# Mixers: the sliding attention's weights moved first, background steps spread over the half units, attended rows multiplied ahead of the recurrent ones

## The chip, the cores and the metric

The kernel runs on one core of a Trainium2 chip. The metric is the time of one execution on the device in microseconds (us); lower is better. Names of engines: PE is TensorE's matmul, DVE is VectorE, ACT is ScalarE, POOL is GpSimd, SP is the queue that issues the transfers.

## What is computed

Two blocks of a language model over 256 positions of width 1024, in float32. The change touches one sublayer of the second block, the mixers: one projection of the normed rows gives the inputs of a sliding window attention and of a gated recurrence, and both results are projected, gated and added.

```python
proj = u @ w_in[layer]
aq, ak, av, rq, rf, ri, rg, ga, gb = jnp.split(proj, splits, axis=-1)
att = sliding_window_attention(aq, ak, av, rel_bias, attn_sinks[layer])   # 8 heads on 2 key heads, window 128
rec = hgrn2_recurrence(rq, rf, ri, lower_bounds[layer])                   # 4 heads, f = lb + (1-lb)*sigmoid(rf)
rec = rms_norm(rec, rec_norm[layer]).reshape(B, S, REC_V_W) * jax.nn.sigmoid(rg)
y_a = att @ w_att_proj[layer]
y_b = rec @ w_rec_proj[layer]
merged = jax.nn.sigmoid(ga) * y_a + jax.nn.sigmoid(gb) * y_b
h = h + merged @ w_out[layer]
```

## The kernel before

All weights stream through the core once, as 528 half units of 128x1024 numbers. A float32 product is made of three matmuls of rounded parts (high by high, high by low, low by high), so each half unit is split first: ACT copies it to `whi` (line 634), DVE subtracts to get `wlo` (line 1109). There are four slots for split half units (`NSPLIT`), so the split of half unit v+3 starts when PE has finished half unit v-1 (`Ahead.upto`). One half unit of the usual kind is 24 matmuls (line 1799).

The mixers begin at half unit 398. Counted from there, in the kernel before: 0 to 3 give the forget gates f of the recurrence, 4 to 7 its queries q, 8 to 11 the attention's queries aq, 12 and 13 its keys ak and values av, 14 to 17 the recurrence's values ii (12 matmuls of 512 columns each), 18 to 37 are ten pairs of gates (`sgm`, `sgr`), 38 to 45 project both results, and 46 to 53 are `w_out`. A pair of half units fills one bank of PSUM, and ACT evicts it when both are done (sigmoid for f and the gates, copy for the others); DVE turns the sigmoid of f into f and 1-f (lines 1718 and 1720).

Beside these run three background tasks: `recurrence()` (on DVE scans, then sixteen rounds of `pp` at line 1605 and `gg` at line 1608, whose `pp` PE sums by the matmuls with `eo_t` at line 1802), `sliding()` (four rounds: PE scores, DVE adds the bias and takes maxima, ACT exponentials at line 989, DVE normalizes at line 1688, PE transposes at line 2281, ACT copies them at line 998, PE multiplies by the values, ACT and DVE store `hhi` and `hlo` at lines 1003 and 1694), and `later()` (the recurrence's states, its output, the norm at line 1648 and the gate at line 1656). Each engine has its own generator of every task; a call `bg.fill(n)` advances the tasks in turn by n steps, and the generators are written so that step number k means the same on each engine. ACT and DVE call `bg.fill` after they have split what `half_unit(v)` asks for, that is half unit v+3:

```python
def half_unit(u, n=1):
    use(u)
    ahead.done = u
    bg.fill(n)
```

PE calls it where the text says. In `pair()` of the kernel before that is behind each of the two half units, and in the loop over the gates four more behind the pair, on all engines alike. What is left of the tasks when the last pair is done is drained by `bg.drain()`, with no matmuls of weights between, and then the projections start: for each output tile 12 matmuls with the attended rows `hhi`/`hlo` and 12 with the recurrent ones `xhi`/`xlo`, which wait for `m_rlo`.

Of the kernel before, what the change touches and what calls it, by code (L numbers as in the profile page):

```python
# [134 lines left out]
def program(nc, w, rows, cols, pT, b1c, ssm_s, ssm_b, ssm_c, ssm_cc, oh, idn, eo, x, out, scr):  # L135
# [4 lines left out]
    with ctx:  # L140
# [484 lines left out]
        def scalar(a):  # L625
# [293 lines left out]
            def mixers():  # L919
                v0, done = [MIX_AT], set()  # L920

                def pair():
                    half_unit(v0[0])
                    half_unit(v0[0] + 1)
                    v0[0] += 2
                    return v0[0]
# [82 lines left out]
                for j in range(2):  # L1009
                    q.wait_ge(s_used, pair())  # L1010
                    a.activation(fq[:, 2 * j:2 * j + 2, :], two(pair_bank(n)), ACT.Sigmoid).then_inc(m_sf, 1)
                    n += 1
                for j in range(2):
                    q.wait_ge(s_used, pair())
                    a.activation(qq[:, 2 * j:2 * j + 2, :], two(4 + n % 2), ACT.Copy)
                    a.activation(gg[:, 2 * j:2 * j + 2, :], two(4 + n % 2), ACT.Copy).then_inc(m_q, 1)
                    n += 1
                bg.add(recurrence())
                for j in range(2):
                    q.wait_ge(s_used, pair())  # L1020
                    a.activation(turned(flat4(aq[:, 2 * j:2 * j + 2, :])), in128(PS[:, 4 + n % 2, :]), ACT.Copy).then_inc(m_aq, 1)
                    n += 1
# [9 lines left out]
                bg.add(sliding())  # L1032
                for c in range(4):
                    half_unit(v0[0], 2)
                    v0[0] += 1
# [4 lines left out]
                for j in range(8):  # L1040
                    while j < 2 and "d" not in done:
                        bg.fill()
                    if j in (4, 6):
                        q.wait_ge(s_used, pair())
# [3 lines left out]
                    q.wait_ge(s_used, pair())  # L1048
# [50 lines left out]
        def vector(v):  # L1099
# [442 lines left out]
            def mixers():  # L1542
                v0, done = [MIX_AT], set()

                def pair():
                    half_unit(v0[0])
                    half_unit(v0[0] + 1)
                    v0[0] += 2
# [163 lines left out]
                v.memset(s_eo[:, 63:64], 0.0).then_inc(m_zero, 1)  # L1712
                for j in range(2):
# [12 lines left out]
                half_unit(v0[0])  # L1726
                half_unit(v0[0] + 1, 0)
                v0[0] += 2
                bg.add(sliding())
                for c in range(4):  # L1730
                    half_unit(v0[0], 2)
                    v0[0] += 1
                bg.add(later())
                for j in range(8):
                    while j < 2 and "d" not in done:
                        bg.fill()
                    if j in (4, 6):
                        pair()
                        bg.fill(4)
                    pair()  # L1740
                    bg.fill(4)
                done.add("rg")
# [51 lines left out]
        def tensor(pe):  # L1794
# [59 lines left out]
            def half_unit(u, o):  # L1854
# [5 lines left out]
                e.then_inc(s_used, 1)  # L1860
# [287 lines left out]
            def mixers():  # L2148
                u0, done, nb = [MIX_AT], set(), [0]

                def bank_free(n):

                    n -= 2
                    if n >= 0:
                        s, c = ((m_sf, n + 1) if n < 2 else (m_q, n - 1) if n < 4 else (m_aq, n - 3) if n < 6 else
                                (m_ak, 1) if n == 6 else (m_av, 1) if n == 7 else None) if n < 8 else (
# [3 lines left out]
                def pair():  # L2160
                    b = pair_bank(nb[0])
                    bank_free(nb[0])
                    nb[0] += 1
                    if nb[0] == 1:
                        first_half_unit(u0[0], PS[:, b, 0:S], 9)
                    else:
                        half_unit(u0[0], PS[:, b, 0:S])
                    bg.fill()
                    half_unit(u0[0] + 1, PS[:, b, S:2 * S])
                    bg.fill()  # L2170
                    u0[0] += 2

                def recurrence():
                    for i in range(7):
# [122 lines left out]
                for _ in range(4):  # L2297
                    pair()
                q.wait_ge(l_eo, 16)
                q.wait_ge(m_f, 8)  # L2300
                q.wait_ge(m_zero, 1)
                mm(PS[:, 3, 0:S], zero.to_broadcast([128, 128]), fq[:, 0, :], True, True)
                bg.add(recurrence())
# [4 lines left out]
                bg.fill()  # L2308
# [14 lines left out]
                bg.add(sliding())  # L2323
                for c in range(4):
# [10 lines left out]
                    e.then_inc(s_used, 1)  # L2335
                    bg.fill(2)
                bg.add(later())
                for j in range(8):
                    while j < 2 and "d" not in done:
                        bg.fill()  # L2340
                    if j in (4, 6):
                        pair()
                        bg.fill(4)
                    pair()
                    bg.fill(4)
                done.add("rg")
                bg.drain()
                for j in range(8):
                    hi, lo = (z.rearrange("p (m k n) -> p m k n", m=2, k=4) for z in weight(u0[0]))
                    u0[0] += 1  # L2350
                    b = 4 + j % 4
                    if j < 2:
                        q.wait_ge(m_sg, 7 + j)
                    elif j >= 4:
                        q.wait_ge(m_gm, j - 3)
                    q.wait_ge(a_ol, 12)
                    for m, (ahi, alo) in enumerate(((hhi, hlo), (xhi, xlo))):
                        if m:
                            q.wait_ge(m_rlo, 1)
                        o = PS[:, b, S * m:S * m + S]  # L2360
                        for k in range(4):
                            mm(o, hi[:, m, k, :], ahi[:, k, :], k == 0, False)
                            mm(o, hi[:, m, k, :], alo[:, k, :], False, False)
                            e = mm(o, lo[:, m, k, :], ahi[:, k, :], False, k == 3)
                    e.then_inc(s_used, 1)
# [36 lines left out]
def pack(i):  # L2402
# [42 lines left out]
    for m in (rf, rq):  # L2445
        for j in range(2):
            ws(cut(m, 2 * j), cut(m, 2 * j + 1))
# [3 lines left out]
    ws(ak, av)  # L2451
    rows_(ri, 512)
# [86 lines left out]
```

## Time and profile before

| | before |
|---|---|
| median of 3 runs | 1823.16 us (1822.29 to 1826.94) |
| the profiled execution | 1826.12 us, span 1824.3 us |
| mean granted clock of TensorE | 0.984 |
| PE busy | 1734.6 us (95%) |
| DVE busy | 1090.7 us (60%) |
| ACT busy | 881.3 us (48%) |
| first matmul of the mixers' half units | 1360.04 us |
| first matmul of the projections | 1532.10 us |

The profiled execution took 1826.12 us by the clock of the runs; the span is what the trace covers of it, from its first instruction to its last. Times of the trace count from the span's start. Busy shares are shares of the span. The granted clock is 1 at 2.4 GHz and 0.5 at 1.2 GHz.

### The profile page before, as it was taken

The numbers are of one execution on the slowest core, as the hardware profiler recorded it, in microseconds if no ns is written. First come the engines' busy times: TensorE is split into PE (matmuls) and PEld (weight loads), VectorE is DVE, ScalarE is ACT, GpSimd is POOL, SyncE is SP. The second block draws the span as 40 slices with busy tenths as digits, with TensorE's granted clock in tenths as the row PEclk, the third lists the DMA queues.
The fourth block names the chain that finished last, engine by engine and source line by source line (L and its number), as shares of the span: only waits on it lengthen the run. The fifth ranks groups of instructions, "written<-read, shape, count | busy, mean of one in ns | idle before, by whom it ended". The sixth has DMA issues, their size and how long they took to land.

```text
span 1824.3 us, 28207 instructions
## 1 busy us (share of the span) xinstructions
PE 1734.6 (95%) x11999; PEld 1588.3 (87%) x11999; DVE 1090.7 (60%) x1410; ACT 881.3 (48%) x1370; POOL 166.6 (9%) x192
## 2 busy tenths in 40 slices
PE   7999999999998999999999998999999997999996
PEld 6899799899977998989789997899989887899994
DVE  5455567678766544658565555655566575655554
ACT  5344466544564455453454445544454444444443
POOL 0000001218001002800000000000000000000000
PEclk9999999999999999999999999999999998999998
DMA  6655433454544544531445554465544331455551
GB/s 226 237 188 187 178 139 139 160 190 179 199 158 153 182 170 143 185 116 47 184 155 176 187 199 146 163 221 184 185 159 177 122 111 70 158 206 185 185 185 69
DMA packets 51086, 300.99 MB, mean 165 GB/s; under 512 B 6073, under 2 KB 12689, under 8 KB 17169
## 3 DMA queue, kind: packets, MB, share of 16 engines
q1 hardware_dynamic: 50800, 298.66, 45.7%
q8 instruction: 95, 1.56, 0.3%
q0 software_dynamic: 160, 0.52, 0.1%
q14 instruction: 31, 0.25, 0.0%
HBM read 298.08 MB, written 1.09 MB: 164 GB/s over the span
## 4 chain that ended last, share of the span: by engine, by line
PE 75%; ACT 9%; DVE 7%; DMA 3%; issue 2%; POOL 1%; SPq 1%; DVEq 0%; ACTq 0%; POOLq 0%
PE PS L1799 72%; DVE wlo L1109 3%; ACT whi L634 3%; DMA raw<-in_w 2%; PE PS L1802 2%; ACT wk L677 2%; POOL st L526 1%; DVE xn L1194 1%; ACT SC L766 1%; PE PS L1919 1%; DVE X L1186 1%; ACT SC L854 1%; DMA SC<-in_pT 0%; POOL st L519 0%; PE PS L2099 0%
## 5 line engine op out<-in xcount | busy, mean ns | idle before, releaser
L1109 DVE TENSOR_TENSOR wlo<-raw,whi 128x1024 fp32r<-128x1024 f32 x528 | 661.3, 1262 | 445.3 <-ACT whi L634 444.5
L634 ACT ACTIVATE whi<-raw 128x1024 fp32r<-128x1024 f32 x528 | 549.7, 1053 | 412.6 <-PE PS L1799 254.3
L1799 PE MATMUL PS<-xhi,whi 128*128 128x256 f32 x2536 | 724.9, 286 | 5.8 <-DVE wlo L1109 5.2
L1799 PE MATMUL PS<-xhi,wlo 128*128 128x256 f32 x2536 | 719.3, 284 | 0.0
L1799 PE MATMUL PS<-xlo,whi 128*128 128x256 f32 x2536 | 710.3, 283 | 0.0
L1799 PEld LDWEIGHTS PS<-xhi,whi 128*128 128x128 f32 x2536 | 489.6, 193 | 14.1 <-DVE wlo L1109 7.0
L1799 PEld LDWEIGHTS PS<-xhi,wlo 128*128 128x128 f32 x2536 | 489.7, 193 | 0.0
L1799 PEld LDWEIGHTS PS<-xlo,whi 128*128 128x128 f32 x2536 | 484.2, 192 | 2.0
L1799 PE MATMUL PS<-whi,hhi 128*128 128x512 f32 x544 | 170.2, 394 | 2.5 <-DVE wlo L1109 2.5
L1799 PE MATMUL PS<-wlo,hhi 128*128 128x512 f32 x544 | 168.5, 391 | 0.0
L1799 PE MATMUL PS<-whi,hlo 128*128 128x512 f32 x544 | 168.3, 390 | 0.0
L716 ACT ACTIVATE wk<-PS 128x256 f32<-128x256 f32 x132 | 50.3, 381 | 164.1 <-PE PS L1799 163.9
L1799 PEld LDWEIGHTS PS<-wlo,hhi 128*128 128x128 f32 x544 | 102.4, 188 | 22.1
L1799 PEld LDWEIGHTS PS<-whi,hlo 128*128 128x128 f32 x544 | 102.4, 188 | 22.0
L1799 PEld LDWEIGHTS PS<-whi,hhi 128*128 128x128 f32 x544 | 98.1, 190 | 19.1 <-DVE wlo L1109 2.7
L1230 DVE TENSOR_TENSOR wk<-PS,wk 128x256 f32<-128x256 f32 x132 | 55.8, 422 | 87.4 <-ACT wk L716 87.3
L519 POOL TENSOR_SCALAR st<-st 128x1 f32<-128x1 f32 x36 | 11.4, 318 | 1055.9 <-ACT wk L677 546.6
L720 ACT ACTIVATE hhi<-wk 128x256 fp32r<-128x256 f32 x132 | 55.2, 418 | 95.8 <-DVE wk L1230 95.8
L1232 DVE TENSOR_TENSOR hlo<-wk,hhi 128x256 fp32r<-128x256 f32 x132 | 58.8, 446 | 63.9 <-ACT hhi L720 63.9
L1799 PE MATMUL PS<-whi,xhi 128*128 128x512 f32 (+2 forms) x272 | 90.5, 391 | 6.2 <-DVE wlo L1109 5.7
L1799 PE MATMUL PS<-wlo,xhi 128*128 128x512 f32 (+2 forms) x272 | 88.1, 382 | 0.0
L1799 PE MATMUL PS<-whi,xlo 128*128 128x512 f32 (+2 forms) x272 | 80.0, 371 | 0.0
(261 smaller groups left out, 1454.7 us busy)
## 6 DMA issues: line engine op xcount, KB each, us to landing
raw<-in_w SPq DMA_DIRECT2D x264, 1024.0 KB, 4.8
gr<-in_rows SPq DMA_DIRECT2D x23, 512.0 KB, 3.8
SC<-scratch SPq DMA_DIRECT2D x1, 2048.0 KB, 12.1
SC<-scratch SPq DMA_DIRECT2D x2, 1024.0 KB, 11.7
X<-in_x SPq DMA_DIRECT2D x2, 512.0 KB, 4.9
xn<-in_sc SPq DMA_DIRECT2D x2, 512.0 KB, 6.8
out<-xn SPq DMA_DIRECT2D x2, 512.0 KB, 2.7
SC<-in_pT SPq DMA_DIRECT2D x3, 256.0 KB, 4.1
```

What stands on the lines that cost most here:

```text
L526: g.tensor_tensor(r, ms, mh[:, 0:max(n, 1)], ALU.pow).then_inc(done, 1)
L634: a.activation(whi[:, u % NSPLIT, :], raw[:, u // 2 % NRAW, u % 2 * HU:u % 2 * HU + HU], ACT.Copy).then_inc(s_hi, 1)
L677: a.activation(wk[:, f], X[:, h, f], ACT.Square, scale=1 / 32, accum_out=ss[:, i:i + 1]).then_inc(s_sq, 1)
L716: a.activation(sg[:, f % 2, :], PS[:, b, 0:S], ACT.Silu).then_inc(s_silu, 1)
L720: a.activation(hhi[:, f % 4, :], hf[:, f % 2, :], ACT.Copy).then_inc(s_hhi, 1)
L766: e = a.activation(pr[:, m, l:z], sc[:, m, l:z], ACT.Exp, bias=n4[:, m, c:c + 1], accum_out=s4[:, m, c:c + 1])
L854: e = a.activation(cst[r, k, :, s, 16 * i:16 * i + 16], o[k][r], ACT.Copy)
L1109: v.tensor_tensor(wlo[:, u % NSPLIT, :], src, hi.bitcast(f32), SUB).then_inc(s_lo, 1)
L1230: v.tensor_tensor(hf[:, f % 2, :], PS[:, up_bank(f), S:2 * S], sg[:, f % 2, :], MUL).then_inc(s_hm, 1)
L1232: v.tensor_tensor(hlo[:, f % 4, :], hf[:, f % 2, :], hhi[:, f % 4, :].bitcast(f32), SUB).then_inc(s_hlo, 1)
L1799: return pe.matmul(o, l, r, start=start, stop=stop)
L1802: return pe.matmul(o, l, r, start=False, stop=True, skip_group_check=True)
```

## The change

The half units of the mixers come in another order (the weights are packed so on the host): aq, ak and av first (0 to 5), then f (6 to 9), q (10 to 13), ii (14 to 17), and the rest as before. `sliding()` is added to the background after half unit 5 and `recurrence()` after the f pairs. From then on there are two background steps in each half unit instead of one, three in each half unit of ii instead of two, and in the loop over the gates three in each half unit and one behind the pair (seven a pair where there were six). On PE they no longer stand behind the half unit but within it. After the loop PE multiplies the attended rows of three output tiles before it waits for the recurrent ones.

```diff
 def mixers():
-    def pair():
-        half_unit(v0[0])
-        half_unit(v0[0] + 1)
+    def pair(a=2, b=2):
+        half_unit(v0[0], a)
+        half_unit(v0[0] + 1, b)
...
     for c in range(4):
-        half_unit(v0[0], 2)
+        half_unit(v0[0], 3)
...
-                        bg.fill(4)
-                    q.wait_ge(s_used, pair())
+                        bg.fill()
+                    if j == 6:
+                        done.add("rg")
+                    q.wait_ge(s_used, pair(3, 3))
...
-                    bg.fill(4)
-                done.add("rg")
+                    bg.fill()
...
-            def half_unit(u, o):
+            def half_unit(u, o, fills=()):
...
                 for k in range(8):
                     mm(o, hi[:, k, :], xhi[:, k, :], k == 0, False)
                     mm(o, hi[:, k, :], xlo[:, k, :], False, False)
                     e = mm(o, lo[:, k, :], xhi[:, k, :], False, k == 7)
-                e.then_inc(s_used, 1)
+                    if k == 7:
+                        e.then_inc(s_used, 1)
+                    if k in fills:
+                        bg.fill()
...
-                def pair():
+                def pair(a=(3, 7), b=(3, 7)):
...
-                for _ in range(4):
-                    pair()
...
-                bg.add(recurrence())
                 pair()
                 pair()
...
                 bg.add(sliding())
+                pair()
+                pair()
+                bg.add(recurrence())
+                pair()
+                pair()
...
                     if j in (4, 6):
-                        pair()
-                        bg.fill(4)
-                    pair()
-                    bg.fill(4)
-                done.add("rg")
+                        pair((2, 5, 7), (1, 3, 5))
+                        bg.fill()
+                    if j == 6:
+                        done.add("rg")
+                    pair((2, 5, 7), (1, 3, 5))
+                    bg.fill()
                 bg.drain()
...
+                q.wait_ge(a_ol, 12)
+                for j in range(3):
+                    if j < 2:
+                        q.wait_ge(m_sg, 7 + j)
+                    projected(j, 0)
+                q.wait_ge(m_rlo, 1)
+                for j in range(8):
+                    if j >= 4:
+                        q.wait_ge(m_gm, j - 3)
+                    if j > 2:
+                        projected(j, 0)
+                    projected(j, 1).then_inc(s_used, 1)
```

First place: DVE, from the split of the last queries on. L1109 is the split of a half unit, L1718 and L1720 make f and 1-f, L1559 begins the recurrence. Before, splits stand with nothing between them and then the recurrence begins:

```order
L1718 TENSOR_SCALAR SC<-SC,st 128x256
L1720 TENSOR_SCALAR SC<-SC 128x256
L1109 TENSOR_TENSOR wlo<-raw,whi 128x1024 x5
L1559 COPY wk<-SC 128x1024
L1561 MEMSET wk 128x64
```

In the changed kernel, where lines are one higher up to the sliding task and seven higher behind it in DVE's mixers, the softmax of the first sliding round (L1684 to L1689) stands between the two pairs of f:

```order
L1110 TENSOR_TENSOR wlo<-raw,whi 128x1024
L1684 TENSOR_TENSOR st<-st 128x4
L1686 RECIPROCAL st<-st 128x4
L1689 TENSOR_TENSOR SC<-SC,st 128x2x256
L1689 TENSOR_TENSOR SC<-SC,st 128x2x128
L1110 TENSOR_TENSOR wlo<-raw,whi 128x1024
L1725 TENSOR_SCALAR SC<-SC,st 128x256
L1727 TENSOR_SCALAR SC<-SC 128x256
```

The first sliding round thus shares DVE and ACT with the gates f, where it stood before beside ii and the first gates.

Second place: PE at the end of the mixers' background. Before, these rows stand between the last gate matmul and the first projection (L2281 transposes of the sliding task, L2256 of the recurrence's output, L1802 its sums):

```order
L1799 MATMUL PS<-xhi,wlo 128x256
L2281 MATMUL PS<-idt,SC 128x128 x6
L1802 MATMUL PS<-SC 128x128 x4
L1799 MATMUL PS<-SC 64x128 x6
L1799 MATMUL PS<-SC 128x256
L1799 MATMUL PS<-SC 128x128
L1799 MATMUL PS<-SC 128x256
L1799 MATMUL PS<-SC 128x128
L2256 MATMUL PS<-idt,xn 128x128 x8
L2281 MATMUL PS<-idt,SC 128x128 x6
L1799 MATMUL PS<-SC 64x128 x6
L1799 MATMUL PS<-hhi,whi 128x256
```

In the changed kernel the last background row of PE (L2264 is L2256 of before) has gate matmuls on both sides, and 54 more follow before the projections:

```order
L1801 MATMUL PS<-xhi,whi 128x256
L1801 MATMUL PS<-xlo,whi 128x256
L1801 MATMUL PS<-xhi,wlo 128x256
L2264 MATMUL PS<-idt,xn 128x128 x4
L1801 MATMUL PS<-xhi,whi 128x256
L1801 MATMUL PS<-xlo,whi 128x256
```

Nothing is left for the drain there.

Third place: PE in the second half unit of a gate pair. A sum of the recurrence (L1804 with `eo_t`) stood behind the 24 matmuls; now it stands behind the sixth or twelfth of them, or in the first half unit of a pair behind the ninth, eighteenth or last:

```order
L1801 MATMUL PS<-xhi,wlo 128x256
L1804 MATMUL PS<-SC,eo_t 32x8x2 x8
L1801 MATMUL PS<-xhi,whi 128x256
L1801 MATMUL PS<-xlo,whi 128x256
L1801 MATMUL PS<-xhi,wlo 128x256
```

This one stands behind the twelfth. On DVE the operation that it waits for stands where it stood, behind the split of the half unit three further on.

## Rows read from the trace of the kernel before

**Rows 1.** The page, first part: busy time of each engine.

```profile
PE 1734.6 (95%) x11999; PEld 1588.3 (87%) x11999; DVE 1090.7 (60%) x1410; ACT 881.3 (48%) x1370; POOL 166.6 (9%) x192
```

**Rows 2.** Busy time by stretch: stretch, its length, PE, PEld, DVE, ACT, POOL, clock, DMA.

```profile
1360.04:1513.31 153.27, 149.12 (x1403) 138.00 (x1403) 101.88 (x162) 71.96 (x108) 0.00 (x0) 0.98 0.38 134
1513.31:1532.10 18.79, 9.13 (x63) 7.07 (x61) 7.88 (x22) 8.90 (x34) 1.85 (x2) 0.73 0.01 1
```

**Rows 3.** Timeline of PE, the drain: start, length, and idle time before with its releaser.

```profile
1524.12 1.12 PE L2256 MATMUL PS<-idt,xn 128*128 128x128 f32 x4 [3.29 <-DVE xn L1648]
...
1532.10 0.55 PE L1799 MATMUL PS<-hhi,whi 128*128 128x256 f32 x1 [1.03 <-DVE hlo L1694]
```

**Rows 4.** Timeline of PE, its other waits in the mixers.

```profile
1422.73 0.60 PE L2208 MATMUL PS<-idt,xn 128*128 128x128 f32 x4
1425.38 0.34 PE L1802 MATMUL PS<-SC,eo_t 128*32 128x8 f32 x16 [2.05 <-DVE SC L1605]
...
1467.99 0.51 PE L1802 MATMUL PS<-SC,eo_t 128*32 128x80 f32 x16 [0.67 <-DVE SC L1605]
...
1509.48 0.79 PE L1802 MATMUL PS<-SC 128*128 128x128 f32 x5 [1.44 <-DVE SC L1638]
```

**Rows 5.** The chain that ended last: two half units of 24 matmuls.

```profile
1426.52 4.36 PE PS L1799 x24
1431.15 3.07 PE PS L1799 x24
```

**Rows 6.** Timeline of ACT.

```profile
1416.92 0.21 ACT L986 ACTIVATE st<-st 128x4 f32<-128x4 f32 x1 [0.94 <-DVE st L1680]
...
1418.79 1.05 ACT L1038 ACTIVATE SC<-PS 128x512 f32<-128x512 f32 x2
...
1463.10 1.28 ACT L1045 ACT_TABLE_LOAD   x1
...
1477.92 1.06 ACT L634 ACTIVATE whi<-raw 128x1024 fp32r<-128x1024 f32 x1 [3.84 <-PE PS L1799]
```

**Rows 7.** Timeline of DVE.

```profile
1367.43 0.41 DVE L1718 TENSOR_SCALAR SC<-SC,st 128x256 f32<-128x256 f32 x1 [0.59 <-ACT SC L1011]
...
1368.74 1.22 DVE L1109 TENSOR_TENSOR wlo<-raw,whi 128x1024 fp32r<-128x1024 f32 x1
...
1399.21 2.29 DVE L1579 TENSOR_TENSOR_SCAN xn<-wk,SC 128x1024 f32<-128x1024 f32 x1
...
1424.11 1.03 DVE L1688 TENSOR_TENSOR SC<-SC,st 128x512 f32<-128x512 f32 x2
...
1479.01 1.23 DVE L1109 TENSOR_TENSOR wlo<-raw,whi 128x1024 fp32r<-128x1024 f32 x1 [0.56 <-ACT whi L634]
1480.15 1.02 DVE L1605 TENSOR_TENSOR SC<-SC 128x832 f32<-128x832 f32 x1
...
1486.73 1.08 DVE L1605 TENSOR_TENSOR SC<-SC 128x896 f32<-128x896 f32 x1
```

**Rows 8.** Timeline of PE: background steps behind half units of the gates.

```profile
1477.75 0.56 PE L1802 MATMUL PS<-SC,eo_t 128*32 128x96 f32 x16
...
1481.30 1.15 PE L1799 MATMUL PS<-SC 128*64 128x128 f32 x12
...
1488.03 0.61 PE L1802 MATMUL PS<-SC,eo_t 128*32 128x112 f32 x16
```

**Rows 9.** Groups by line: busy us, mean ns; the sixteen `pp` operations.

```profile
L1605 DVE TENSOR_TENSOR SC<-SC 128x64 f32<-128x64 f32 (+15 forms) x16 | 11.5, 721 | 0.0
```

**Rows 10.** The projections: second output tile on PE, splits on DVE.

```profile
1536.65 0.28 PE L1799 MATMUL PS<-hhi,whi 128*128 128x256 f32 x1
1536.77 0.28 PE L1799 MATMUL PS<-hlo,whi 128*128 128x256 f32 x1
...
1539.43 1.23 DVE L1109 TENSOR_TENSOR wlo<-raw,whi 128x1024 fp32r<-128x1024 f32 x1 [0.52 <-ACT whi L634]
...
1558.03 1.23 DVE L1109 TENSOR_TENSOR wlo<-raw,whi 128x1024 fp32r<-128x1024 f32 x1 [0.52 <-ACT whi L634]
```

More of the change, by code:

```diff
@@ L1010, in mixers @@
                     q.wait_ge(s_used, pair())
[L1011 to L1021 removed]
+                    a.activation(turned(flat4(aq[:, 2 * j:2 * j + 2, :])), in128(PS[:, pair_bank(n), :]), ACT.Copy).then_inc(m_aq, 1)
                     n += 1
@@ L1032, in mixers @@
                 bg.add(sliding())
+                for j in range(2):
+                    q.wait_ge(s_used, pair())
+                    a.activation(fq[:, 2 * j:2 * j + 2, :], two(4 + n % 2), ACT.Sigmoid).then_inc(m_sf, 1)
+                    n += 1
+                bg.add(recurrence())
+                for j in range(2):
+                    q.wait_ge(s_used, pair())
+                    a.activation(qq[:, 2 * j:2 * j + 2, :], two(4 + n % 2), ACT.Copy)
+                    a.activation(gg[:, 2 * j:2 * j + 2, :], two(4 + n % 2), ACT.Copy).then_inc(m_q, 1)
+                    n += 1
                 for c in range(4):
-                    half_unit(v0[0], 2)
+                    half_unit(v0[0], 3)
                     v0[0] += 1
@@ L1712, in mixers @@
                 v.memset(s_eo[:, 63:64], 0.0).then_inc(m_zero, 1)
+                pair()
+                pair()
+                half_unit(v0[0])
+                half_unit(v0[0] + 1, 0)
+                v0[0] += 2
+                bg.add(sliding())
                 for j in range(2):
@@ L1725, in mixers @@
                 pair()
[L1726 to L1729, printed above, removed]
                 for c in range(4):
-                    half_unit(v0[0], 2)
+                    half_unit(v0[0], 3)
                     v0[0] += 1
@@ L2295, in sliding @@
                         yield
-                for _ in range(4):
[L2298 to L2303, printed above, removed]
                 pair()
@@ L2323, in mixers @@
                 bg.add(sliding())
+                pair()
+                pair()
+                bg.add(recurrence())
+                pair()
+                pair()
                 for c in range(4):
@@ L2341, in mixers, with projected @@
                     if j in (4, 6):
[L2342 to L2346, printed above, removed]
-                bg.drain()
[L2348 to L2351, printed above, removed]
+                        pair((2, 5, 7), (1, 3, 5))
+                        bg.fill()
+                    if j == 6:
+                        done.add("rg")
+                    pair((2, 5, 7), (1, 3, 5))
+                    bg.fill()
+                bg.drain()
+                def projected(j, m):
+                    hi, lo = (z.rearrange("p (m k n) -> p m k n", m=2, k=4)[:, m] for z in weight(u0[0] + j))
+                    ahi, alo = ((hhi, hlo), (xhi, xlo))[m]
+                    o = PS[:, 4 + j % 4, S * m:S * m + S]
+                    for k in range(4):
+                        mm(o, hi[:, k, :], ahi[:, k, :], k == 0, False)
+                        mm(o, hi[:, k, :], alo[:, k, :], False, False)
+                        e = mm(o, lo[:, k, :], ahi[:, k, :], False, k == 3)
+                    return e
+                q.wait_ge(a_ol, 12)
+                for j in range(3):
                     if j < 2:
                         q.wait_ge(m_sg, 7 + j)
-                    elif j >= 4:
+                    projected(j, 0)
+                q.wait_ge(m_rlo, 1)
+                for j in range(8):
+                    if j >= 4:
                         q.wait_ge(m_gm, j - 3)
[L2356 to L2365, printed above, removed]
+                    if j > 2:
+                        projected(j, 0)
+                    projected(j, 1).then_inc(s_used, 1)
                 q.wait_ge(m_rec, 2)
@@ L2451, in pack @@
     ws(ak, av)
+    for m in (rf, rq):
+        for j in range(2):
+            ws(cut(m, 2 * j), cut(m, 2 * j + 1))
     rows_(ri, 512)
```

40 lines of the change are left out of this document (20 added, 20 removed).

## The prediction

> **What bounds the kernel now.** I read the page first: PE is busy 95% of the span, DVE 60%, ACT 48% [rows 1]. So what counts is when PE waits or runs at half clock; work of the others counts where PE waits for it. Then the busy time by stretch. The mixers up to the projections take 172.1 us, from 1360.0 to 1532.1, of which the last 18.8 are the drain, where PE is busy 9.13 us at a mean clock of 0.73 [rows 2]. The timeline of PE shows who is late there: the longest wait, 3.29 us, is for DVE's norm, the last for `hlo` [rows 3]. 9.13 us at 0.73 are 6.7 us of work at full clock, so the drain loses 18.8 - 6.7 = 12.1 us. The first output tile behind it is still slow: it takes 1536.65 - 1532.10 = 4.55 us [rows 3, 10] where 24 matmuls without a background step take 2.88 (0.12 us from one to the next [rows 10]; with a step behind them 3.07 [rows 5]), so 1.7 more. Before the drain PE waits only three times: 2.05, 0.67 and 1.44 us [rows 4]; behind the first, 24 matmuls took 4.36 instead of 3.07 us [rows 5], so that wait costs 3.3. The change can win back 12.1 + 1.7 + 3.3 + 0.7 + 1.4 = 19.2 us at most.
>
> **The change part by part.**
>
> *The drain* goes: PE's last background step now stands before the last 54 gate matmuls. Behind the loop the recurrent rows need ACT's eviction of the last gate (0.5), `xhi` (about 1.06, as a `whi` of the same size [rows 6]), and `xlo` (1.2, as a `wlo` [rows 7]), 3.2 us with the handovers; the 36 attended matmuls put ahead of them take 4.3 us. So no wait: the cover has 1.1 us to spare. I count all 19.2 us as won.
>
> *More interruptions.* A background step among 24 matmuls costs 3.07 - 2.88 = 0.18 us beside its own work. In the order of before 21 places on PE have background work between weight matmuls (the drain apart), in the changed order 43. 22 x 0.18 = 4.0 us lost. No matmul is added or removed otherwise, no transfer is moved to another place of SP's queue, and ACT loads its tables as often (nine times in the mixers).
>
> *First sliding round.* Let S be the start of half unit 6, where it now begins. PE: scores behind 12 matmuls, done at S+2.4; half unit 6 ends at S+3.9 and 8 at S+9.7, where the transposes stand. DVE and ACT: the bias is added by S+3.5 (768 elements, 0.95 us as 832 take 1.02 [rows 7]); then DVE splits half unit 10, which waits for the end of 6: `whi` begins 0.17 us behind it (1477.92 against 1477.75) [rows 6, 8] and lasts 1.06, `wlo` lets DVE go 1.14 later (1479.01 to 1480.15) [rows 7], so 2.4 us behind a half unit's end, S+6.3. Maxima and sink, 1.4: S+7.75. Exponentials, 1.87 (1416.92 to 1418.79) [rows 6]: S+9.7. Behind them ACT's queue has the sigmoid of the first f pair with its table, 1.28 [rows 6] and 0.5 (half of a `whi`'s 1024 elements): S+11.5, and DVE's queue has the four operations on f, 1.31 (1367.43 to 1368.74) [rows 7], then the split of 11 (1.14), and only then the softmax, 1.4 with its last 1.03 [rows 7]: S+15.4, on PE S+15.7. PE waits 6.0 us. Before, this softmax ended at 1425.1 [rows 7], behind half unit splits and two evictions, and PE's 2.05 us of wait [rows 4] were for the same queue; its transposes then stood twice as many matmuls behind the scores. A wait of 2.05 was followed by 1.3 us of half clock [rows 4, 5]; I add that: 7.3.
>
> *Second sliding round*, now beside the recurrence's scans. From the start of half unit 12 DVE has: split of 15 behind an eviction 3.35, bias 0.9, scan 2.3, split 1.15, maxima 0.95, copies 0.9, split 1.15, sink 0.4, memsets and second scan 2.6 (its 2.29 [rows 7]), softmax 1.4, in all 15.1 us. PE reaches the transposes, in half unit 15, behind 2 x 2.88 + 2.84 + 2.13 = 10.7 us. It waits 4.6, and 1.3 for the clock: 5.9. Rounds three and four have more steps between, and I find no wait there.
>
> *The sixteen rounds of the recurrence.* This is the largest term. Round k needs `pp` of k, 0.27 to 1.22 us (mean 0.72 [rows 9]). DVE gets to it 2.4 us behind the end of the half unit before (2.9 where ACT evicts a pair first), behind whatever background step comes ahead of it there. In the kernel before PE is never there sooner: in the first half unit of a pair it comes behind 24 matmuls and some 3 us of steps that follow the pair (1481.30 to 1488.03, with `pp` done at 1487.8) [rows 7, 8]; the spare is 0.2 us. In the changed kernel PE is there 1.2, 2.4 or 3.0 us into the first half unit, or 0.8, 1.5, 2.3 or 3.0 into the second. Example: round 11 stands behind six matmuls of a second half unit, at 0.8; DVE: 2.4 + 0.88 + 0.06 = 3.35; PE waits 2.55. Followed round by round through the order with these durations, the waits are 0.45, 1.5, 2.15, 2.05, 0, 0, 0.4, 0, 1.95, 1.55, 2.55, 0, 1.8, 0.55, 0.95, 0: together 15.9. Then the copies of A3 (1.5, as now 1.44 [rows 4]) and the norm of the recurrence's output, now 30 matmuls behind its product where squares, POOL and norm need 5 to 6 us: 2.0. Sum 19.4 us. The bounds: 0, if DVE is always ready; 16 x 2.55 + 3.5 = 44, if every round waits as long as the worst. I take the walk's value, since each of its terms is a duration of a row.
>
> *Projections.* The first three tiles now end 1.44 us apart, the first at 4.3 + 1.44 = 5.8 us. Per tile DVE takes (1558.03 - 1539.43)/5 = 3.72 us and splits half unit 42 by 4.0 us behind the first tile's end [rows 10]; so half unit 47 is split at 5.8 + 4.0 + 5 x 3.72 = 28.4, and PE wants it at 8 x 2.88 + 2.84 = 25.9: 2.5 us lost. (Before, the first tile ended at 4.55 and PE wanted it 1.7 later, which just fitted.)
>
> *Sum*: -19.2 + 4.0 + 7.3 + 5.9 + 19.4 + 2.5 = **+19.9 us**. Against the profiled execution's 1826.1 that is 1846; the median of the runs lies 3.0 below it, so 1843. About 0.3%, 5.5 us, is what a measurement of this kernel can tell from no change.
>
> **The rivals.**
>
> *The steps are ready in time* (faster). Were all new waits zero, the sum would be -19.2 + 4.0 = -15.2, or -12.7 with the projections' 2.5: 1808 to 1811. For it: DVE is busy 102 of 153 us in the stretch and PE waits 4 us there [rows 2]. Against: DVE's free time lies before its split, which waits for PE. It decides below 12.7 us of new waits, against my 7.3 + 5.9 + 19.4 = 32.6. Chance 0.1.
> The Trainium skill, Perfetto Trace Analysis, Optimization Strategy, says that interleaving regimes with different contended engines may improve performance; by that this rival is what happens. Rows 2 and 3 agree that the drain is such a regime, and no row here says that the interleaving stays free.
>
> *Both halves cancel* (same). The first two sliding waits come but the recurrence's are a third of mine, or the reverse: 1818 to 1828. Chance 0.09.
>
> *The clock falls too* (slower still). Seven of my waits in the gates are 1.5 us or more, and a wait of 2.05 was followed by half clock while one of 1.44 was not [rows 4, 5]. At 1.3 each: +9, 1852. For it: they come one or two a pair. Against: slow matmuls give DVE time, so part of it shortens the next wait. Chance 0.18.
> The Trainium skill, TensorE: Matmul & The Clock Gate, A second HAM failure mode, says that frequent short idles between groups of matmuls can make the clock swing between its levels; by that the 1852 would be the forecast. The drain's 0.73 agrees, the stretch before it with 0.98 holds no such group of waits.
>
> *My forecast*, 1834 to 1848: chance 0.63.
>
> **How the numbers follow.** Faster is the first rival, 0.1; within 0.3% the second, 0.09; slower the other two, 0.81. The likeliest one's range is 1834 to 1848. For 8 in 10 it reaches up into the clock rival, 1855, and down through the cancelling one to 1822, since both bounds of the largest term are far off.
>
> **What would show it.** After the change PE's timeline should have no drain: gate matmuls up to the first `hhi` one, and no wait on `m_rlo`. It should have a wait of about 6 us for the softmax at the first sliding transposes, one of 3 to 5 at the second, and some ten waits of 0.4 to 2.6 us for `pp` inside half units of the gates, the mean clock there below 0.98. From the first matmul of the mixers to the first projection some 189 us instead of 172. Wrong would be: DVE's splits sooner behind a half unit's end than 2.4 us, or `pp` done before PE's ninth matmul. The step I trust least is the size of the recurrence's term.

## The result and the profile after

The changed kernel took 1850.6 us (median of 4 runs, 1845.63 to 1853.69) against 1824.42 for the kernel before beside it: ratio 1.014, 95% interval 1.011 to 1.0171, so 26.2 us slower. The forecast was 1843, likeliest 1834 to 1848, range 1822 to 1855. The profiled execution took 1853.69 us, span 1851.9.

First the sections of the page on busy time, and the waits of PE from the mixers' first matmul to the first projection (who waited for whom: us in total, times, longest), of the changed kernel:

```profile
PE 1744.5 (94%) x11999; PEld 1592.2 (86%) x11999; DVE 1090.1 (59%) x1410; ACT 878.8 (47%) x1369; POOL 166.6 (9%) x192
...
PE PS L1804 <- DVE SC L1606: 14.6, 11, 2.6
PE PS L2289 <- DVE SC L1689: 10.0, 2, 5.9
PE PS L2264 <- DVE xn L1649: 2.2, 1, 2.2
PE PS L1804 <- DVE SC L1639: 1.8, 1, 1.8
```

The counts are those of [rows 1], ACT's less one (a table load: eight in the mixers, where the prediction had nine as before); PE is busy 10 us longer with the same 11999 matmuls. The drain is gone, and 28.6 us of waits stand in the mixers, where before 4.2 stood ahead of the drain ([rows 4]) and 9.7 in it. Busy time by stretch, with the columns of [rows 2]:

```profile
1360.11:1440.00 79.89, 69.48 (x569) 64.28 (x568) 47.66 (x79) 36.84 (x61) 0.00 (x0) 0.93 0.35 125
1440.00:1500.00 60.00, 48.68 (x454) 42.38 (x445) 29.15 (x51) 19.75 (x31) 0.00 (x0) 0.87 0.25 88
1500.00:1560.44 60.44, 53.53 (x453) 48.12 (x451) 32.43 (x57) 21.26 (x47) 1.85 (x2) 0.93 0.22 78
1560.44:1610.32 49.88, 47.12 (x295) 41.63 (x293) 32.96 (x44) 21.01 (x29) 0.85 (x2) 1.00 0.50 181
```

From the first matmul to the first projection the mixers take 200.33 us (1360.11 to 1560.44) instead of 172.06; the forecast was 189. The granted clock, 0.98 up to the drain in [rows 2], is 0.87 to 0.93 over all three stretches. Behind the first projection 49.88 us follow to the next sublayer's first transposes; before they were 48.64. How the clock falls is to be seen in the timeline of PE, second half of a gate pair:

```profile
1444.53 0.34 PE L1804 MATMUL PS<-SC,eo_t 128*32 128x16 f32 x16 [1.67 <-DVE SC L1606]
...
1447.18 0.28 PE L1801 MATMUL PS<-xlo,whi 128*128 128x256 f32 x1
1447.31 0.28 PE L1801 MATMUL PS<-xhi,wlo 128*128 128x256 f32 x1
1449.67 0.35 PE L1804 MATMUL PS<-SC,eo_t 128*32 128x24 f32 x16 [2.08 <-DVE SC L1606]
...
1450.43 0.42 PE L1801 MATMUL PS<-xhi,whi 128*128 128x256 f32 x1
1450.64 0.42 PE L1801 MATMUL PS<-xlo,whi 128*128 128x256 f32 x1
1450.86 0.41 PE L1801 MATMUL PS<-xhi,wlo 128*128 128x256 f32 x1
...
1453.83 0.28 PE L1801 MATMUL PS<-xhi,whi 128*128 128x256 f32 x1
1453.94 0.28 PE L1801 MATMUL PS<-xlo,whi 128*128 128x256 f32 x1
...
1457.38 0.42 PE L1801 MATMUL PS<-xlo,whi 128*128 128x256 f32 x1
1457.60 0.41 PE L1801 MATMUL PS<-xhi,wlo 128*128 128x256 f32 x1
```

Up to the second wait one matmul follows the other by 0.12 to 0.13 us, 0.7 us behind it by 0.21 to 0.22: the lower level of the clock. From 1453.83 the distance is 0.12 again, and behind the next wait, of 2.09 us up to 1456.79, it is 0.21 to 0.22 once more. So the level comes and goes with the waits. What PE waits for is in the chain that ended last (start, length, what):

```profile
1451.92 0.85 PE PS L2216 x4
1452.77 1.23 PE PS L1801 x6
...
1454.08 1.07 ACT whi L634
...
1455.21 1.11 issue
1456.32 0.43 DVE SC L1606
...
1456.79 0.36 PE PS L1804 x14
```

PE ends a half unit, ACT and DVE split the next but two into the slot that came free, then DVE makes `pp`, then PE goes on: the loop of 2.4 us plus `pp` that the prediction walked through. (The 1.11 of "issue" are the split by DVE, L1110 in its timeline.)

### The profile page after: what moved, and what is told of

The parts are those of the page before. It is cut to its first block, busy times and chain, and to the rows that moved or that the text cites. A ratio compares the mean times of both kernels' runs of the same rounds, so it can differ in the third digit from the quotient of the medians.

```text
span 1851.9 us, 28207 instructions
## 1 busy us (share of the span) xinstructions
PE 1744.5 (94%) x11999; PEld 1592.2 (86%) x11999; DVE 1090.1 (59%) x1410; ACT 878.8 (47%) x1369; POOL 166.6 (9%) x192
## 4 chain that ended last, share of the span: by engine, by line
PE 67%; DVE 11%; ACT 10%; DMA 5%; issue 4%; POOL 1%; SPq 1%; DVEq 0%; ACTq 0%; POOLq 0%
PE PS L1801 64%; DVE wlo L1110 5%; ACT whi L634 4%; DMA raw<-in_w 4%; PE PS L1804 2%; ACT wk L677 2%; DVE xn L1195 1%; POOL st L526 1%; ACT SC L766 1%; PE PS L1925 1%; DMA SC<-in_pT 1%; DVE X L1187 1%; DVE SC L1348 1%; ACT SC L854 1%; DVE wk L1231 0%
## 5 line engine op out<-in xcount | busy, mean ns | idle before, releaser
L1110 DVE TENSOR_TENSOR wlo<-raw,whi 128x1024 fp32r<-128x1024 f32 x528 | 661.4, 1262 | 485.7 <-ACT whi L634 484.6
```

What stands on the lines that cost most here:

```text
L1110: v.tensor_tensor(wlo[:, u % NSPLIT, :], src, hi.bitcast(f32), SUB).then_inc(s_lo, 1)
```

## The experiments

Each kernel was timed against the kernel before on its own chip; its ratio holds against that. "Stretch" is the time from the mixers' first matmul to the first projection in the profiled execution, which is one execution out of several: the changed kernel's took 3.1 us more than its median, those of fill_gates and fill_all 3.0 and 4.1 us less than theirs. Their mixers also begin 4.0 us sooner, which the stretch leaves out. So where a stretch carries a conclusion, the ratio stands beside it.

| kernel | median us | ratio, 95% interval | stretch us | waits for `pp` us |
|---|---|---|---|---|
| before | 1824.42 | 1 | 172.06 | 2.7 |
| changed | 1850.6 | 1.014 [1.011, 1.0171] | 200.33 | 14.6 |
| late_round | 1829.54 | 1.0029 [1.0016, 1.0042] | 173.33 | 1.3 |
| steps_behind | 1827.71 | 1.0015 [1.0, 1.0029] | 175.29 | 4.0 |
| order_only | 1839.66 | 1.0084 [1.0054, 1.0113] | 186.65 | 14.3 |
| fills_only | 1849.97 | 1.0141 [1.0118, 1.0164] | 199.54 | 16.2 |
| order_turned | 1831.11 | 1.0032 [1.0019, 1.0045] | 177.54 | 10.5 |
| late_slow | 1824.75 | 1.0002 [0.9991, 1.0014] | 170.09 | 0.6 |
| late_both | 1829.26 | 1.0027 [1.0016, 1.0038] | 174.48 | 3.9 |
| hh_only | 1826.76 | 1.0011 [1.0001, 1.0021] | 171.26 | 2.7 |
| fill_gates | 1845.6 | 1.0114 [1.0099, 1.013] | 192.63 | 3.3 |
| fill_all | 1842.59 | 1.0093 [1.0077, 1.0108] | 188.82 | 3.3 |
| late_tail | 1829.85 | 1.0027 [1.0017, 1.0037] | 172.80 | 2.6 |
| slow_old | 1824.45 | 0.9994 [0.9982, 1.0006] | 171.59 | 0.6 |

**Are the recurrence's rounds the loss?** The changed kernel with one empty step of PE more ahead of its sixteen rounds, so that each sum stands a turn of the tasks (18 to 24 matmuls) further behind its `pp`:

```diff
                     done.add("B")
                     yield
+                    yield
                     for s in range(15, -1, -1):
```

> The changed kernel with one more empty step on PE ahead of the recurrence's sixteen rounds, so that PE sums a round one turn of the tasks (21 matmuls, 2.5 us, and the steps between) later than DVE makes its pp; nothing is left out. My theory (PE meets each round sooner than DVE's queue can reach it, behind the split of the half unit three further on): the 14.6 us of waits for pp in the gates fall below 2 us, and most of the half clock in the gates goes with them (some 8 us), so about 1828 us, 1822 to 1835. Rival a (the clock is low in the gates because of the two sliding waits ahead of them): waits fall by 14, the clock does not change, about 1837. Rival b (DVE is simply short of time there and the waits come back at the next thing it owes): 1845 or more.

Measured: ratio 1.0029, 21 us of the 26 back. PE's waits and the stretches of the gates:

```profile
PE PS L2290 <- DVE SC L1689: 10.0, 2, 5.9
PE PS L1804 <- DVE SC L1606: 1.3, 1, 1.3
PE PS L1804 <- DVE SC L1639: 1.0, 1, 1.0
PE PS L2265 <- DVE xn L1649: 1.0, 1, 1.0
...
1360.93:1440.00 79.07, 69.02 (x557) 64.03 (x558) 47.76 (x79) 36.86 (x61) 0.00 (x0) 0.91 0.36 127
1440.00:1500.00 60.00, 58.68 (x628) 51.72 (x627) 42.18 (x76) 28.23 (x47) 0.00 (x0) 1.00 0.29 106
1500.00:1534.26 34.26, 32.20 (x283) 29.56 (x281) 19.06 (x32) 12.83 (x31) 1.85 (x2) 1.00 0.33 114
```

The waits of rounds, copies and norm fall by 15.3 us (18.6 to 3.3), the stretch by 27.0, and the clock in the gates is 1.00. So some 12 us come from more than the waits. The sliding waits (10.0 us) stay, as they must.

**Is it the place within the half unit, or the number of steps?** The same steps at the same half units, but all behind them on PE:

```diff
-                def pair(a=(3, 7), b=(3, 7)):
+                def pair(a=(7, 7), b=(7, 7)):
...
-                    pair((2, 5, 7), (1, 3, 5))
+                    pair((7, 7, 7), (7, 7, 7))
```

> The changed kernel with its background steps on PE put behind the half units again (two behind each of the early ones, three behind each of ii, three behind each half unit of the gates and one behind the pair), same numbers of steps, same order of weights; nothing is left out. My theory: PE comes to a round 3.0 us or more into the half unit instead of 0.8 to 3.0, so the waits for pp fall from 14.6 to 3 to 6 us and the clock's loss with them, while the first sliding wait (its transposes stand behind the same half unit as now) stays at 6 and the second at 3.5 to 4: about 1834 us, 1828 to 1840. Rival (it is the number of steps, seven a pair instead of six, that DVE cannot follow, not their place): 1845 to 1852.

Measured: ratio 1.0015, just below the theory's range. The waits for `pp` fall to 4.0 us in three rounds. So in this order the places within the half units cost 23 of the 26 us, and the numbers of steps alone bring no such loss.

**The order alone and the places alone.** order_only is the changed kernel with the step numbers and places of before and the old loop over the output tiles; fills_only has the order of before, with the changed kernel's steps and places and the old loop.

```diff
order_only, against the changed kernel
-                    bg.fill(3)
+                    bg.fill(2)
...
-                    pair((2, 5, 7), (1, 3, 5))
-                    bg.fill()
+                    pair((7,), (7,))
+                    bg.fill(4)
fills_only, against the kernel before
-                    pair()
-                    bg.fill(4)
+                    pair((2, 5, 7), (1, 3, 5))
+                    bg.fill()
```

> Only the first part of the change: the sliding attention's half units first and the sliding task from half unit 6 on, but with the numbers and places of the background steps of the kernel before (one behind each half unit, two behind those of ii, four more behind a pair of gates) and its projections; nothing is left out. My theory: the first sliding transposes stand five half units behind the scores instead of two and a half, 14.4 us against the 13.3 that DVE and ACT need, so no wait of 6 us; eight more steps are done before the gates' end than in the kernel before, so the drain is shorter by a third: about 1817 us, 1811 to 1823. Rival (the early place beside f and the scans is itself the trouble, at any rate of steps): a wait of 4 us or more at a sliding transpose, 1824 to 1832.

> Only the second part: the kernel before with its order of weights and tasks and its projections, but with the changed kernel's steps (two in each half unit once tasks run, three in each half unit of ii, seven in a pair of gates, on PE within the half units). Nothing is left out. My theory: most of the drain goes, the waits for pp of 13 to 17 us and the clock's loss beside them come, some more interruptions: 1832 to 1845 us, about 1838. Rival (the rounds wait only because the sliding task went first and loads DVE): waits for pp below 5 us, 1815 to 1822.

Measured: 1.0084 and 1.0141. The steps' numbers and places together bring as much as the whole change, also without the new order; that was expected at 1832 to 1845 and came to 1850. But the order alone was expected at 1811 to 1823 and costs 15 us; here I was wrong. Each half costs by itself and the two don't add up, so neither can be called the whole cause. With the same order, more steps and the new loop, steps_behind costs only 3 us. The sliding rounds of order_only don't wait, as expected; PE's waits are others:

```profile
PE PS L1802 <- DVE SC L1605: 14.3, 11, 3.6
PE PS L2261 <- DVE xn L1648: 5.2, 2, 3.4
```

fills_only also waits in places of its own, once 5.5 us for a scan (L1590) and twice, 4.8 in all, for the states (L1630), so its loss is not the changed kernel's wait by wait. That these come from before's order, which starts the sliding task in the midst of the recurrence, was not tested.

**Why did the order alone cost?** The tasks take turns. In the kernel before the list is recurrence, sliding, later; adding sliding first turns it, so that both of the recurrence's rounds of a gate pair fall behind its second half unit (in the trace of order_only rounds three and four, five and six and so on stand behind the same gate matmul). The same kernel with the recurrence first again:

```diff
+                bg.tasks.insert(0, bg.tasks.pop())
                 bg.add(later())
```

> The kernel with only the order changed (sliding attention's weights and steps first, numbers and places of steps as before, the old projections), with the turn of the background tasks set so that behind the first half unit of a pair stands the recurrence's step, as in the kernel before. My theory of why that kernel came out at 1839.7 instead of 1817: both the recurrence's rounds of a pair stood behind its second half unit, where DVE is only just done with its split; with the turn of before the some 14 us of waits for DVE's products go down to under 4: 1818 to 1828. Rival: the place in a pair makes no difference, and what costs is that sliding rounds three and four, with their work on DVE, run into the gates' first pairs; the waits stay at 12 to 15 us and the time at 1835 to 1842.

Measured: ratio 1.0032 with 10.5 us of waits for `pp`. That is between the two: the stretch is 9.1 us shorter, but seven rounds still wait, the first for 2.9 us. The turn of the tasks is about six tenths of what the order cost (9.1 of 14.6 us of stretch); which of the other shifts makes the rest was not singled out.

**Is it the clock that my sum is short of?** The waits stay, but PE is kept at work in them: ahead of eleven rounds, as many 128-column matmuls as fill the wait measured there. fill_all has 49 and 34 more ahead of the two sliding transposes. The spare matmuls write, with a start flag, to columns that nobody reads, in the bank that the rounds accumulate in. In these two kernels the output comes out otherwise; that the flag is the reason was not shown by a run of its own. They serve for their times alone.

```diff
+DUMMY = {1: 2, 2: 13, 3: 17, 4: 17, 7: 2, 9: 16, 10: 4, 11: 21, 13: 11, 14: 3, 15: 9}
...
+                        for _ in range(DUMMY.get(16 - s, 0)):
+                            mm(PS[:, 3, 384:512], xhi[:, 0, 0:128], xhi[:, 0, 128:256], True, True)
                         q.wait_ge(m_pp, 16 - s)
```

> The changed kernel with spare 128-column matmuls ahead of PE's waits for DVE's products in eleven of the recurrence's rounds, as many as fill the wait that its trace shows there (2 to 21, about 0.118 us each, 115 in all; their result goes to unused columns of a bank and nobody reads it). The waits as such stay, but PE is not idle in them. My theory: the 9 us or so by which the changed kernel's first projection comes later than my sum of waits says are half-clock spells that the idle stretches bring about; with them filled the granted clock from 1440 to 1560 us goes from 0.87 and 0.93 to 0.98 or more, some idle waits come back since PE is sooner at the next round, and the time falls by 4 to 9 us: 1842 to 1847. Rival: DVE's pace sets the rounds, whatever PE's clock is; faster matmuls only lengthen the next wait and the time stays at 1849 to 1852, as would it if the clock doesn't depend on the idle stretches.

> The same, and besides 49 and 34 spare matmuls ahead of the two sliding transposes with waits of 5.91 and 4.13 us. My theory: the granted clock from 1383 to 1440 us goes from 0.91 to 0.97 or more, and another 2 to 4.5 us are gained on top of the kernel with the gates' waits filled: 1838 to 1845. Rival: no further gain, or the spare matmuls cost a little, 0 to +2 us on that kernel.

Stretches of both, fill_gates first, with what it still waits for `pp`:

```profile
1356.16:1440.00 83.84, 73.60 (x605) 68.39 (x605) 49.91 (x81) 39.69 (x64) 0.00 (x0) 0.92 0.37 132
1440.00:1500.00 60.00, 56.98 (x594) 51.12 (x597) 33.24 (x62) 20.97 (x37) 0.00 (x0) 1.00 0.22 80
1500.00:1548.79 48.79, 44.46 (x391) 40.89 (x383) 26.38 (x44) 17.26 (x39) 1.85 (x2) 0.97 0.24 85
...
PE PS L1805 <- DVE SC L1607: 3.3, 9, 1.1
```

```profile
1356.14:1440.00 83.86, 82.39 (x729) 77.75 (x728) 51.16 (x85) 40.75 (x66) 0.00 (x0) 0.99 0.37 132
1440.00:1500.00 60.00, 57.24 (x585) 50.94 (x585) 34.07 (x61) 22.91 (x41) 0.00 (x0) 1.00 0.24 89
1500.00:1544.96 44.96, 40.66 (x352) 37.90 (x352) 23.93 (x40) 14.26 (x33) 1.85 (x2) 0.96 0.24 84
```

With more matmuls issued, the kernels get faster: the stretch by 7.7 us with the gates' waits filled (200.33 to 192.63) and by 3.8 more with the sliding ones. The clock is 1.00 from 1440 to 1500 us in both, and 0.99 instead of 0.92 before it only where the sliding waits are filled. Of the 7.7 us, 0.65 stand at the very start of the mixers: there fill_gates' first matmuls ran at the higher level and those of the changed kernel and fill_all at the lower, ahead of any edit. By the medians the ratio goes from 1.014 to 1.0114 to 1.0093, some 5 and 4 us, 8.6 in all where the stretches say 11.5; both medians lie in the ranges expected. The interval of fill_gates overlaps that of the changed kernel, fill_all's just doesn't (1.0108 against 1.011). So the gain of both fillings together is shown, and its size is 8.6 to 11.5 us.

The prediction's 189 us for the stretch is not what its own terms give. The 1.7 us of the first output tile lie behind the first projection, so they are 172.06 - 17.5 + 4.0 + 32.6 = 191.2 with, and 188.6 without, its 2.6 us of half clock. fill_all's 188.82 us, with little half clock left, is to be put beside the 188.6.

**The attended rows ahead, alone.** The kernel before with only the new loop over the output tiles:

```diff
+                q.wait_ge(a_ol, 12)
+                for j in range(3):
+                    projected(j, 0)
+                q.wait_ge(m_rlo, 1)
                 for j in range(8):
...
+                    if j > 2:
+                        projected(j, 0)
+                    projected(j, 1).then_inc(s_used, 1)
```

> The kernel before with one edit of the change: the attended rows' products of the first three output tiles ahead of the recurrent rows'. In this kernel the drain ends with the low part of the attended rows' values, so there is nothing left for the 36 matmuls to hide. My theory: the drain stays at 18.8 us, and the first tiles end 1.44 us apart instead of 2.88, so that PE is at the weights of the later tiles before DVE, whose 3.72 us for a tile set the pace: 0 to 2.5 us of new waits, 1824 to 1827, ratio 1.000 to 1.0015. Rival: the edit gains by itself, since PE does not wait for the recurrent rows' low part; then some 1 to 2 us less, 1821 to 1823.

Measured: ratio 1.0011, 2 us. In the profiled execution the projections take 51.60 us (1532.25 to 1583.85) instead of 48.64. PE's timeline has three waits behind the first tiles, 1.9 us in all:

```profile
1555.05 0.36 PE L1799 MATMUL PS<-hhi,whi 128*128 128x256 f32 x1 [0.62 <-DVE wlo L1109]
...
1558.72 0.70 PE L1799 MATMUL PS<-whi,xhi 128*128 128x512 f32 x2 [0.56 <-issue]
...
1562.40 0.74 PE L1799 MATMUL PS<-whi,xhi 128*128 128x512 f32 x2 [0.68 <-DVE wlo L1109]
```

**Can the order be kept without its waits?** late_slow has the late round and one step a half unit, behind it, in the pairs 6 to 13; late_both keeps two steps there and puts four and two empty steps, on all engines, between exponentials and transposes of the first two sliding rounds.

```diff
late_slow, against late_round
-                def pair(a=(3, 7), b=(3, 7)):
+                def pair(a=(7,), b=(7,)):
late_both, against late_round
+LATER = (4, 2, 0, 0)
...
+                        for _ in range(LATER[j]):
+                            yield
                         q.wait_ge(w_p, 2 * j + 2)
```

> The late round (each of PE's sixteen recurrence rounds one step later than in the changed kernel), and besides one background step instead of two for each half unit of the pairs from 6 to 13, so that the first sliding rounds are spread over more half units. My theory: PE's wait at the first sliding transposes (5.92 us in the late-round kernel) comes from too few matmuls between scores and transposes; with twice as many it is 0 to 1 us, and the second's (4.13) falls or goes too. That is worth 5.9 + 1.3 of clock, up to 4.1 + 1.3 more: 1829.5 becomes 1817 to 1823. Rival: DVE's and ACT's queue moves along with PE, since their steps are spread by the same rule, so that the softmax comes later by as much and the wait stays at 5 to 6 us: 1828 to 1831.

> The late round, and besides four and two empty steps, on all engines, between the exponentials and the transposes of the first and the second sliding round. My theory: with those steps the softmax stands behind more splits on DVE but PE has 24 matmuls more for every step that each places, so the first wait (5.92 us) becomes 0 to 1 and the second (4.13) 0 to 1; with the half clock behind each (1.3 us as the changed kernel's trace has it behind waits above 2 us) 1829.5 - 5.9 - 4.1 - 2.6 = 1817, 1814 to 1821, below the kernel before. Rival: the empty steps only push the sliding work against the recurrence's, whose rounds then wait for DVE again; 1826 to 1834.

Measured: 1.0002 and 1.0027. In both the sliding waits go, from 10.0 us to 0.5 and to none. late_slow's 1824.75 lies between its theory (1817 to 1823) and its rival (1828 to 1831). Its stretch is 2 us below that of before; but PE waits 3.6 us for A3's copies (L1639), 2.7 for the scan (L1590) and 2.5 for the norm, and the new projections take 50.88 us. late_both is its rival's case: new waits of 2.6 (issue), 3.9 (`pp`), 2.3 and 1.3 us stand where there were none.

**The last two.** late_tail moves late_slow's empty step ahead of the products behind the scan and puts another ahead of the product with A3's copies; slow_old is late_slow with the old loop over the output tiles.

```diff
late_tail, in two places
+                    yield
                     q.wait_ge(m_sc, 2)
...
                     while "A" not in done:
                         yield
+                    yield
```

> The changed kernel with one step instead of two for each half unit of the pairs from 6 to 13 and PE's steps behind half units there, and with one empty step more on PE in two places: ahead of the recurrence's pq products (which makes its sixteen rounds one step later too) and ahead of the product with A3's copies. The kernel with slow sliding steps and the late round still waits 2.66 us at the one and 3.57 us at the other place. My theory: both waits go down to under 1 us, and of the 6.2 us some 3 to 5 are gained, since what lies behind the second moves towards the drain: 1820 to 1822, ratio 0.996 to 0.999, below both kernels. Rival: the waits move to the norm's transposes, which stand closer to the end then, and PE's drain comes back; 1824 to 1828.

> The kernel with the late round and slow sliding steps, with the projections' loop of the kernel before (each tile's attended and recurrent rows together). My theory from the kernel with only that loop changed: the new loop costs 2.2 us (48.6 us from the first projection to the next block's transposes become 50.9), since the tiles' pace is DVE's; the old loop gives them back and pays at most 0.6 us for the recurrent rows' low part: 1822 to 1824, ratio 0.998 to 0.9995, below both kernels if only just. Rival: without the attended rows ahead, the end of the mixers waits 1.5 us or more for the recurrent rows and nothing is gained: 1824.5 to 1827.

Measured: 1.0027 and 0.9994. late_tail's two waits went (0.6 us and none), but sliding waits of 3.5 and 1.1, one `pp` wait of 2.6 and 4.5 us for the norm took their place: worse than its rival (1824 to 1828). slow_old was expected at 1822 to 1824, its rival at 1824.5 to 1827; it took 1824.45 beside 1825.79 for the kernel before. It is the only kernel below the one before, and its interval (0.9982 to 1.0006) includes 1. Its timeline shows the wait that the attended rows had hidden, 1.76 us where at most 0.6 was expected:

```profile
1536.50 0.38 PE L1801 MATMUL PS<-xhi,whi 128*128 128x256 f32 x1 [1.76 <-DVE xlo L1747]
```

So no version here is shown to beat the kernel before.

## Why the prediction was right, and where it was short

**Direction and mechanism: right; size: too small.** Slower by over 0.3% had 0.81. The measured 1850.6 lies above the likeliest range, 1834 to 1848, and inside the wide one, which reached up for the clock's sake. Term by term, from the profile after:

| term | forecast us | measured us |
|---|---|---|
| drain and [rows 4] waits | gone | no wait on `m_rlo`, last step between gate matmuls |
| first sliding wait | 6.0 | 5.91 |
| second sliding wait | 4.6 | 4.13 |
| sixteen rounds | 15.9 | 14.6 |
| A3's copies, norm | 1.5, 2.0 | 1.75, 2.21 |
| projections, with the slow start behind the drain | 2.5 - 1.7 | 49.88 - 48.64 = 1.2 |
| half clock behind waits | 2.6 | 11.5 (8.6 by the medians) |

The walk through the rounds names the right ones: eleven rounds wait, the eleven of the forecast. Forecast 2.15 and 2.05 for rounds three and four, measured 2.08 and 2.09; 2.55 for round eleven, measured 2.56. Furthest off is round ten, 1.55 against 0.55. The timeline of PE, three of them:

```profile
1449.67 0.35 PE L1804 MATMUL PS<-SC,eo_t 128*32 128x24 f32 x16 [2.08 <-DVE SC L1606]
...
1456.79 0.36 PE L1804 MATMUL PS<-SC,eo_t 128*32 128x32 f32 x16 [2.09 <-DVE SC L1606]
...
1498.67 0.84 PE L1804 MATMUL PS<-SC,eo_t 128*32 128x88 f32 x16 [2.56 <-DVE SC L1606]
```

And the first sliding wait, in DVE's timeline, comes by the queue that the prediction set out: behind the table load and the sigmoid of f, DVE's four operations, a split, and only then the softmax:

```profile
1392.45 0.41 DVE L1725 TENSOR_SCALAR SC<-SC,st 128x256 f32<-128x256 f32 x1 [3.94 <-ACT SC L1025]
...
1393.75 1.22 DVE L1110 TENSOR_TENSOR wlo<-raw,whi 128x1024 fp32r<-128x1024 f32 x1
...
1395.29 1.03 DVE L1689 TENSOR_TENSOR SC<-SC,st 128x512 f32<-128x512 f32 x2
```

**The term that was mis-sized: the clock.** The forecast charged half clock behind the two sliding waits alone, 1.3 us each. Filling the waits shows what it was: 7.7 us in the gates and 3.8 behind the sliding rounds, 11.5 in all, or 8.6 by the ratios. With 6.0 to 8.9 us more the forecast's 1843 would have been 1849 to 1852. Its rival "the clock falls too" had 9 us in the gates and 1852, and is what happened; I gave it 0.18 because slow matmuls give DVE time. That is seen too, but is small: the 115 spare matmuls at 0.118 us fill 13.6 us, and 3.3 us of waits for `pp` are left. The rounds thus take 16.9 us with the clock up and 14.6 with it down, so the slow matmuls gave back 2.3 us. (The forecast's 15.9 was walked through with the clock up; round ten then has 0.5 us filled and 1.1 left, against 1.55.) What I read too narrowly was [rows 4]: one wait of 1.44 us without half clock behind it, standing alone. Here a wait of 1.67 us had none behind it, and the next of 2.08, 5 us later, did.

The Trainium skill, TensorE: Matmul & The Clock Gate, A second HAM failure mode, tells of a kernel in which frequent short idles between groups of matmuls make the clock swing between its levels. The trace agrees: 0.87 from 1440 to 1500 us, where no wait is longer than 2.6 us, and 1.00 with the same waits filled by matmuls.

**The rival with all steps in time** would need late_round's gates, slow sliding steps and more; the nearest kernel, late_slow, comes to 1.0002. The Trainium skill, Perfetto Trace Analysis, Optimization Strategy, says that interleaving regimes with different contended engines may improve performance. Here no such gain is shown: late_slow has 2 us less in the stretch (170.09 against 172.06) and the ratio 1.0002. What is taken from the drain comes back as waits of one engine's queue for another's.

**What stays open.** Why order_turned still waits 10.5 us; why the order and the steps each cost by themselves and don't add up; and how much of the 0.18 us of each interruption is real. fill_all's stretch, 188.82, is 1.6 us above 172.06 - 17.5 + 4.0 + 28.6 = 187.2. But its clock is still 0.99 and 0.96 in two of its stretches, which I estimate from these two figures at up to 2.6 us, so the 1.6 don't show the term to be short.

## What to carry to other kernels

A background step causes no wait only as long as it stands as far behind its producer as the producer's own queue is long, here 2.4 us plus the operation. When steps are spread, shift the consumer by one step as well: one empty step on PE got back 21 of 26 us. Price such waits as a group, the clock with them: in the gates eleven waits of 0.3 to 2.6 us, 14.6 in all, cost up to 7.7 us more by the half clock behind them.

## What the runs showed of the hardware

- Matmuls whose result nobody uses, issued while PE would wait, made the kernel faster, by 11.5 us in the stretch and 8.6 by the medians: the granted clock from 1440 to 1500 us was 1.00 instead of 0.87.
- After two waits of 1.67 and 2.08 us with a group of dense matmuls between, the clock fell to the lower level 0.7 us into the next group and stayed there for 3.4 us; after the first of them alone it had not.
- The half clock comes and goes with the waits: with the gates' waits gone (late_round) and the sliding ones there, 0.91 to 1440 us is followed by 1.00.
